# Head norms whose sums and roots stand in a 128x256 tile and are spread again by half-array products, the gating read from PSUM, and new sequences for TensorE

## The chip, the cores and the metric

The kernel runs on one core of one Trainium2 chip. The metric is the device time of one execution in microseconds (us), from the first to the last instruction and what the runtime adds around them. TensorE (PE in the profile) multiplies; PEld is its weight load, which can overlap a running product. ScalarE (ACT), VectorE (DVE) and GpSimd (POOL) work beside it, and SyncE (SP) issues the weight transfers.

## The reference

Two blocks follow each other on a sequence of 256 tokens of width 1024. The first block has two layers: a short gated convolution beside a gated DeltaNet of 8 heads (layer 0), and HGRN2 with 16 heads (layer 1). The second block has one mixer with 16 heads of width 64 (softmax attention, mLSTM, block attention) and an MLP of width 2816. All is float32. What the change touches are the norms of heads of width 128 in the first block:

```python
def rms_norm(x, g):
    xf = x.astype(jnp.float32)
    y = xf * lax.rsqrt(jnp.mean(jnp.square(xf), axis=-1, keepdims=True) + NORM_EPS)
    return (y * g.astype(jnp.float32)).astype(x.dtype)

def l2_normalize(x):
    xf = x.astype(jnp.float32)
    return (xf * lax.rsqrt(jnp.sum(jnp.square(xf), axis=-1, keepdims=True) + 1e-6)).astype(x.dtype)
...
    q, k = l2_normalize(q), l2_normalize(k)                                        # layer 0
    o = rms_norm(o, gdn_norm_g) * jax.nn.silu(z_b.reshape(bsz, s, h, GDN_HEAD_DIM)) # layer 0
    o = rms_norm(o, hgrn_norm_g) * jax.nn.silu(heads(z))                            # layer 1
```

## The kernel before

Activations lie with their features on the 128 partitions and the 256 tokens along the free dimension, so one head of width 128 is a tile of 128x256. The weights come in slabs of mostly 1 MB (`RAW`, a ring of 6). Each slab is split into a high and a low part: ScalarE copies it to `WH` (L1386, `split`), VectorE takes the difference to `WL` (L1799). TensorE then makes three products for each pair of a weight and an activation (`products`, L916 is the helper that issues every product: high by high, high by low, low by high). These are the rows with WH and WL; all other products are plain float32, and the trace shows each of those as two instructions.

The program is a list of named steps, such as `gp:0:3:1`. A step has a part on each engine that takes part in it. Each engine runs its parts in an order that is written out by hand in a table: `ORDER_T` for TensorE, `ORDER_S` for ScalarE, `ORDER_V` for VectorE. A part waits for the parts of other engines that it needs; `claim` makes TensorE wait until the last readers of a step's PSUM banks are done. A name that begins with `first:` is the first half of a step's products.

The steps that matter below:

- `norm:k:g`, `norm:q:g` (layer 0, group g of 4 heads, 4 times), `gr:g:p` (layer 0, output norm), `hr:g:p` (layer 1, 4 groups). TensorE multiplies the squares with a 128x128 tile of ones (`ONES`), which sums over the head's features and gives the sum on all 128 partitions: two float32 products of 512 columns for a group of 4 heads, ten groups in all. ScalarE takes ln, exp and a square over these 1024 columns (L1396, L1397, L1402), VectorE makes a Newton step and the product with the values (L1766 to L1768).
- `go`/`ho` make the head outputs in PSUM banks 0 and 1; `gq`/`hq` copy and square them on ScalarE (L1467, L1468); `gz`/`hz` gate them on VectorE.
- `gp`, `gu` and `gx` (layer 0): seven levels of a triangular inverse. `gp` and `gu` of levels 1 to 6 write products of 64 output columns into halves of the array (rows 128\*64), `gx` (L1079) are transposes.
- `hd`, `hm` (layer 1): products of 32 or 64 output columns, `ada`: products with `SCZ`, 32 output columns each, four of them side by side.
- `score:h`, `turn:h`, `pv:h` (second block, 16 heads of width 64): the scores take a 64-partition half of the array by the parity of h (rows 64\*128), the transposes L1307 the whole, `pv` a 64-column half (rows 128\*64).

```python
            def t_norm(step, kind, g):
                pe.wait_ge(scalar_done, scalar_at(kind, g, 1))
                for i in range(2):
                    last = mm(PS[:, step.banks[i], :], ONES[:], SQ[:, i, :])
                last.then_inc(tensor_done, 1)
```

Of the kernel before, what the change touches and what calls it, by code (L numbers as in the profile page):

```python
# [36 lines left out]
P = 128  # L37
# [78 lines left out]
def plan(stage):  # L116
# [165 lines left out]
    def gdn(g):  # L282
# [3 lines left out]
               later(step, "norm", "q", g, on="TSV", banks=(2, 3), readers="V"),  # L286
# [3 lines left out]
        for i in range(NL):  # L290
# [4 lines left out]
            for c in range(NT):  # L295
# [6 lines left out]
                later(step, "go", g, on="T", banks=(0, 1), readers="S", read_in=("gq", g, pieces(g, 2)[-1][0]))]  # L302
        out += [later(step, "gq", g, p, on="S") for p, _ in pieces(g, 2)]
        out += [later(step, "gz", g, on="V")]
        out += [later(step, "gr", g, p, on="TSV", banks=[2 + i for i in pairs], readers="V") for p, pairs in pieces(g, 2)]
        return out

    def norm_k(g):
        return later(step, "norm", "k", g, on="TSV", banks=(0, 1), readers="V")
# [180 lines left out]
gp:1:5:1 gx:1:4:1 gx:1:5:0 gp:1:6:0 gu:1:5:1 gu:1:6:0 gp:1:6:1 gx:1:5:1 gv:1:0 out:0:1:1 gs:1 gu:1:6:1 gks:1 out:0:0:2  # L490
gv:1:1 go:1 gr:1:0 gr:1:1 pl:0:0 out:0:1:2 first:out:0:0:3 first:out:0:1:3 out:0:0:3 out:0:1:3 xt:0:0:0 pl:0:1 ada:0:0
xt:0:0:1 ada:0:1 xt:0:1:0 ada:1:0 ada:1:1 adat:0 xt:0:1:1 first:gate:0:0:0 first:gate:0:0:1 gate:0:0:0 gate:0:0:1
first:gate:0:1:0 adat:1 xt:1:1 xt:1:0 first:gate:0:1:1 gate:0:1:0 gate:0:1:1 ada:2:0 ada:2:1 first:f:0:0 xt:1:3 adat:2
xt:1:2 first:f:0:1 f:0:0 f:0:1 first:q1:0:0 q1:0:0 first:q1:0:1 q1:0:1 first:i:0:0 hd:0 i:0:0 first:f:1:0 hm:0:0
first:i:0:1 hm:0:1 f:1:0 i:0:1 hm:0:2 first:f:1:1 f:1:1 hm:0:3 first:z1:0:0 z1:0:0 hm:0:4 first:z1:0:1 hm:0:5 z1:0:1
hm:0:6 first:q1:1:0 hc:0 q1:1:0 ho:0 first:q1:1:1 q1:1:1 hr:0:0 hd:1 first:i:1:0 first:f:2:0 i:1:0 first:i:1:1 hm:1:0
first:f:2:1 hm:1:1 i:1:1 f:2:0 hm:1:2 f:2:1 hm:1:3 first:z1:1:0 z1:1:0 hm:1:4 first:z1:1:1 z1:1:1 first:q1:2:0 hm:1:5
q1:2:0 hm:1:6 first:q1:2:1 hc:1 q1:2:1 ho:1 first:i:2:0 hr:1:0 hd:2 i:2:0 first:f:3:0 first:i:2:1 i:2:1 f:3:0 hm:2:0
first:f:3:1 first:z1:2:0 hm:2:1 f:3:1 hm:2:2 z1:2:0 hm:2:3 first:z1:2:1 hm:2:4 z1:2:1 hm:2:5 first:q1:3:0 hm:2:6
q1:3:0 hc:2 first:q1:3:1 ho:2 q1:3:1 hr:2:0 first:i:3:0 hd:3 i:3:0 hm:3:0 first:z1:3:0 first:i:3:1 i:3:1 hm:3:1 z1:3:0  # L500
ada:3:0 hm:3:2 first:z1:3:1 hm:3:3 z1:3:1 hm:3:4 ada:3:1 adat:3 hm:3:5 out:1:0:0 hm:3:6 out:1:1:0 hc:3 out:1:0:1 ho:3
out:1:1:1 hr:3:1 hr:3:0 out:1:0:2 pl:1:0 out:1:1:2 first:out:1:1:3 first:out:1:0:3 out:1:0:3 out:1:1:3 xt:2:0:0 pl:1:1
xt:2:0:1 ada:8:0 ada:8:1 xt:2:1:0 xt:2:1:1 ada:6:0 ada:6:1 adat:8 first:gate:1:0:0 first:gate:1:0:1 gate:1:0:0
gate:1:0:1 first:gate:1:1:0 adat:6 first:gate:1:1:1 gate:1:1:0 gate:1:1:1 ada:7:0 ada:7:1 ada:9:0 ada:9:1 ada:4:0
adat:7 xt:4:1 xt:4:0 xt:4:2 xt:4:3 adat:9 ada:4:1 first:feat:8 gates:0 feat:8 gates:1 first:feat:0 qn:1:2 gcol feat:0
first:feat:1 qn:0:0 feat:1 grow:0 first:feat:2 qn:0:1 grow:1 feat:2 first:feat:3 qn:0:2 grow:2 feat:3 first:feat:4
grow:3 first:feat:6 feat:4 first:feat:5 feat:5 grow:4 feat:6 first:feat:7 qn:1:0 feat:7 first:val:0:0 qn:1:1 score:0
val:0:0 first:val:0:1 score:1 score:2 turn:0 val:0:1 first:val:1:0 turn:1 score:3 score:4 pv:0 pv:1 turn:2 val:1:0
turn:3 score:6 score:5 first:val:1:1 turn:4 pv:2 pv:3 score:8 score:7 turn:5 val:1:1 turn:6 pv:4 pv:5 turn:7 score:9
score:10 turn:8 pv:6 pv:7 score:12 score:11 turn:9 pv:8 pv:9 turn:10 score:13 mln turn:11 ada:5:0 ada:5:1 adat:4  # L510
turn:12 pv:10 pv:11 adat:5 score:15 score:14 turn:13 pv:12 pv:13 out2:0:0 turn:14 out2:1:0 turn:15 pv:14 pv:15
first:out2:0:1 first:out2:1:1 out2:0:1 out2:1:1 ada:10:0 ada:10:1 ada:11:0 adat:10 xt:5:0 xt:5:1 xt:5:2 xt:5:3
ada:11:1 ff:0 adat:11 ff:1 ff:2 ff:3 ff:5 ff:4 ff:6 ff:8 ff:7 ff:9 ff:11 ff:10 ff:12 ff:13 ff:14 ff:15 ff:16 ff:17
ff:18 ff:19 ff:21 ff:20 down:0:0 down:0:1 down:0:2 down:0:3 down:0:4 first:down:0:5 down:1:0 down:0:5 down:1:1
down:1:2 down:1:3 down:1:4 first:down:1:5 down:1:5
# [103 lines left out]
def build(nc, wst, x_in, xt_in, pt_in, wba, wga, cst_in, msk_in, vec_in, lnrow, out):  # L619
# [11 lines left out]
    with ctx:  # L631
# [282 lines left out]
        def _(pe):  # L914
# [1527 lines left out]
```

## Time and profile before

| | before |
|---|---|
| median of 3 runs | 1049.68 us (1047.58 to 1049.87) |
| span of the profiled execution | 1048.4 us |
| PE / PEld busy | 1019.6 us (97%) / 897.6 us (86%) |
| DVE / ACT busy | 752.1 us (72%) / 530.2 us (51%) |
| PE's share of the chain that ended last | 87% |

The span of the profiled execution is 1.3 us under the median of the three runs and inside their range; the page gives no other time for it. A product in the trace is longer than the time it occupies TensorE, since the next one starts before its end: what a product occupies is the distance from its start to the start of the next.

### The profile page before, as it was taken

The page shows a single profiled execution, that of the slowest core. Times are in us where ns is not written, and L with a number is a line of the kernel's source. Part 1 is how long each engine was busy: PE and PEld are TensorE (multiplying, and loading weights), DVE is VectorE, ACT ScalarE, POOL GpSimd, SP SyncE. Part 2 cuts the span into 40 slices and gives each one's busy share as a digit, 9 for nine tenths or more (in the row PEclk, how much of TensorE's full clock was granted, in tenths as well). Part 3 has the DMA queues.
Part 4 walks back from the last instruction along what each step waited for, and adds up shares of the span by engine and source line. Part 5 has one row for each costly group of instructions (what it writes and reads, how often), then busy time and mean ns, then how long its engine had stood idle before and what let it go on. Part 6 is the DMA issues. An engine that isn't in the chain of part 4 may idle for free.

```text
span 1048.4 us, 21565 instructions
## 1 busy us (share of the span) xinstructions
PE 1019.6 (97%) x9120; PEld 897.6 (86%) x9120; DVE 752.1 (72%) x1049; ACT 530.2 (51%) x590; POOL 0.5 (0%) x7
## 2 busy tenths in 40 slices
PE   9999999999999999999999999989999999999998
PEld 7999999999866798989898787659986669999986
DVE  5999957678557668677787866867986775565553
ACT  5674544483353464435555433656687564335331
POOL 0000000000000000000000000000000000000000
PEclk8999999999999999999999999999999999999999
DMA  9454343244326664425343554876352446545441
GB/s 353 162 183 161 129 154 106 97 162 161 123 81 255 236 240 167 150 83 200 122 162 122 178 185 163 320 295 241 123 181 99 161 143 260 218 184 188 157 171 47
DMA packets 26302, 181.47 MB, mean 173 GB/s; under 512 B 3040, under 2 KB 3296, under 8 KB 4960
## 3 DMA queue, kind: packets, MB, share of 16 engines
q1 hardware_dynamic: 25056, 174.66, 45.2%
q10 hardware_dynamic: 1152, 5.45, 1.4%
q8 instruction: 73, 1.20, 0.5%
q14 instruction: 21, 0.17, 0.1%
HBM read 179.04 MB, written 1.05 MB: 172 GB/s over the span
## 4 chain that ended last, share of the span: by engine, by line
PE 87%; DVE 7%; ACT 3%; DMA 2%; issue 1%; SPq 0%; DVEq 0%; ACTq 0%
PE PS L916 84%; DVE WL L1799 2%; DMA RAW<-wst 1%; ACT WH L1386 1%; PE PS L1079 1%; DMA layer<-xt 1%; DVE X L1995 1%; DVE X L1996 1%; PE PS L1157 1%; PE PS L1307 0%; DVE STAT L1977 0%; DVE X L1976 0%; DVE layer_ln L2109 0%; DVE layer L2102 0%; ACT block L1690 0%
## 5 line engine op out<-in xcount | busy, mean ns | idle before, releaser
L916 PE MATMUL PS<-XTH,WH 128*128 128x256 f32 x1392 | 403.7, 290 | 6.2 <-issue 1.5
L916 PE MATMUL PS<-XTL,WH 128*128 128x256 f32 x1392 | 394.8, 284 | 0.0
L916 PE MATMUL PS<-XTH,WL 128*128 128x256 f32 x1392 | 394.7, 284 | 0.0
L1799 DVE TENSOR_TENSOR WL<-RAW,WH 128x2048 fp32r<-128x2048 f32 x138 | 314.2, 2277 | 99.8 <-ACT WH L1386 96.4
L1386 ACT ACTIVATE WH<-RAW 128x2048 fp32r<-128x2048 f32 x138 | 262.7, 1904 | 214.2 <-PE PS L916 208.7
L916 PEld LDWEIGHTS PS<-XTH,WH 128*128 128x128 f32 x1392 | 267.8, 192 | 12.6 <-issue 3.8
L916 PEld LDWEIGHTS PS<-XTL,WH 128*128 128x128 f32 x1392 | 268.0, 193 | 1.6 <-issue 1.4
L916 PEld LDWEIGHTS PS<-XTH,WL 128*128 128x128 f32 x1392 | 267.8, 192 | 0.0
L916 PE MATMUL PS<-WH,YH 128*128 128x512 f32 x224 | 89.6, 400 | 1.1 <-DVE YL L2274 1.1
L916 PE MATMUL PS<-WH,YL 128*128 128x512 f32 x224 | 87.4, 390 | 0.0
L916 PE MATMUL PS<-WL,YH 128*128 128x512 f32 x224 | 87.3, 390 | 0.0
L916 PE MATMUL PS<-WH,XTH 128*128 128x512 f32 x160 | 64.3, 402 | 0.9 <-ACT MROW L1569 0.8
L916 PE MATMUL PS<-WL,XTH 128*128 128x512 f32 x160 | 62.5, 390 | 0.0
L916 PE MATMUL PS<-WH,XTL 128*128 128x512 f32 x160 | 62.5, 390 | 0.0
L916 PEld LDWEIGHTS PS<-WH,YH 128*128 128x128 f32 x224 | 42.1, 188 | 10.6 <-DVE YL L2274 1.3
L916 PEld LDWEIGHTS PS<-WL,YH 128*128 128x128 f32 x224 | 42.1, 188 | 9.0 <-issue 0.7
L916 PEld LDWEIGHTS PS<-WH,YL 128*128 128x128 f32 x224 | 42.0, 188 | 8.9
L916 PEld LDWEIGHTS PS<-layer 128*32 128x32 f32 (+2 forms) x1920 | 39.5, 119 | 10.2 <-issue 4.7
L1734 ACT ACT_TABLE_LOAD x36 | 46.2, 1283 | 0.8
L916 PE MATMUL PS<-layer 128*32 128x16 f32 (+3 forms) x1920 | 44.3, 198 | 1.9 <-DVE layer L2104 1.2
L1718 ACT ACTIVATE mlp<-PS 128x256 f32<-128x256 f32 x22 | 8.4, 384 | 67.0 <-PE PS L916 55.2
L916 PEld LDWEIGHTS PS<-WH,XTH 128*128 128x128 f32 x160 | 30.1, 188 | 8.0 <-ACT MROW L1569 1.0
(293 smaller groups left out, 1112.6 us busy)
## 6 DMA issues: line engine op xcount, KB each, us to landing
RAW<-wst SPq DMA_DIRECT2D x162, 1024.0 KB, 4.9
LNW<-lnrow ACTq DMA_DIRECT2D x3, 1024.0 KB, 6.7
RAW<-wst SPq DMA_DIRECT2D x4, 512.0 KB, 5.7
layer<-xt SPq DMA_DIRECT2D x2, 512.0 KB, 5.3
XR<-x ACTq DMA_DIRECT2D x1, 1024.0 KB, 4.7
out<-X SPq DMA_DIRECT2D x4, 256.0 KB, 3.3
CST<-cst ACTq DMA_DIRECT2D x1, 640.0 KB, 8.7
PT<-pt SPq DMA_DIRECT2D x1, 512.0 KB, 5.6
```

Of the source, the lines that this page charges most:

```text
L916: return pe.matmul(o, lhsT, rhs, start=start, stop=stop)
L1079: last = pe.transpose(PS[:, 2 + c, h * P:(h + 1) * P], U[:, c * HG + h, :], ident)
L1157: last = pe.transpose(PS[:, step.banks[0], o:o + P], src[:, c, k * P:(k + 1) * P], ident)
L1386: fn(WH[:, k % SPLIT_RING, 0:n], RAW[:, i % RAW_RING, 0:n], ACT.Copy).then_inc(scalar_done, 1)
L1718: fn(SG[:, j % 2, :], PS[:, bank_of("ff", j), 0:T], ACT.Silu).then_inc(scalar_done, 1)
L1734: act.preload_act_table_set(wanted)
L1799: tt(WL[:, i % RAW_RING, 0:n], RAW[:, i % RAW_RING, 0:n], as_float(WH[:, k % SPLIT_RING, 0:n]), ALU.subtract).then_inc(vector_done, 1)
L1995: link(stt(X[:, c, s], X[:, c, s], AGG[:, c, 0:1], LNW[:, 0, s], ALU.subtract, ALU.mult))
L1996: stt(X[:, c, s], X[:, c, s], RSTD[:, c:c + 1], LNW[:, 1, s], ALU.mult, ALU.add).then_inc(vector_done, 1)
```

## The change

The sum over a head's features is now written by products with 32 columns of ones into one quarter of the output partitions for each of the 4 heads: four products of 256 columns into one 128x256 tile (`head_sums`). ScalarE and VectorE take the root there, over 256 columns and not 1024. A new TensorE step (`spread:k:g`, `spread:q:g`, `grs:g`, `hrs:g`) brings each head's root back to all 128 partitions, by four products of 256 columns whose contraction runs over 64 partitions, in turn over the lower and the upper half, the lower half's into one bank and the upper half's into another. VectorE then multiplies by the spread roots, read from PSUM. The head outputs are no longer copied by ScalarE, which only squares them (`head_squares`); VectorE gates them from PSUM (`head_outputs`). `ORDER_T` is rewritten nearly throughout, in the second block's attention too; `ORDER_S` and `ORDER_V` change where these steps stand.

```diff
+            def head_sums(bank, squares):
+                for h in range(HG):
+                    last = mm(PS[h * QUAD:(h + 1) * QUAD, bank, 0:T], ONES[:, 0:QUAD], squares(h))
+                return last
+
+            def spread(o, roots):
+                for a in range(2):
+                    for b in range(2):
+                        r, s = slice(b * HD, (b + 1) * HD), b * HD + a * QUAD
+                        pick = ident[r, s:s + 1].to_broadcast([HD, P])
+                        last = mm(o(2 * b + a), pick, roots[r, :])
+                return last
 ...
             def t_norm(step, kind, g):
                 pe.wait_ge(scalar_done, scalar_at(kind, g, 1))
-                for i in range(2):
-                    last = mm(PS[:, step.banks[i], :], ONES[:], SQ[:, i, :])
-                last.then_inc(tensor_done, 1)
+                head_sums(step.banks[0], lambda h: SQ[:, h // 2, h % 2 * T:(h % 2 + 1) * T]).then_inc(tensor_done, 1)
+
+            def t_spread(step, kind, g):
+                pe.wait_ge(cst_loaded, 16)
+                pe.wait_ge(vector_done, vector_at("norm", kind, g))
+                spread(lambda h: PS[:, step.banks[h // 2], h % 2 * T:(h % 2 + 1) * T], NR).then_inc(tensor_done, 1)
 ...
-            def t_hr(step, g, p):
-                pe.wait_ge(scalar_done, scalar_at("hq", g, p))
-                for i in dict(pieces(g, HGRN_GROUPS))[p]:
-                    last = mm(PS[:, 2 + i, :], ONES[:], tiles(HS, 2 * i, 2))
-                last.then_inc(tensor_done, 1)
+            def t_hr(step, g):
+                for c in range(NT):
+                    pe.wait_ge(scalar_done, scalar_at("hq", g, c))
+                head_sums(2, lambda h: HS[:, h, :]).then_inc(tensor_done, 1)
+
+            def t_hrs(step, g):
+                pe.wait_ge(vector_done, vector_at("hr", g))
+                spread(lambda h: PS[:, step.banks[h // 2], h % 2 * T:(h % 2 + 1) * T], HS[:, 2, :]).then_inc(tensor_done, 1)
 ...
             def s_norm(kind, g):
                 act.wait_ge(tensor_done, tensor_at("norm", kind, g))
-                b = bank_of("norm", kind, g)
-                rsqrt_and_square(flat(SQ), R2[:], PS[:, b:b + 2, :].rearrange("p b n -> p (b n)"), 1.0, 1).then_inc(scalar_done, 1)
+                rsqrt_and_square(NY, N2, PS[:, bank_of("norm", kind, g), 0:T], 1.0, 1).then_inc(scalar_done, 1)
 ...
-            def s_hq(g, p):
+            def s_hq(g, c):
                 act.wait_ge(tensor_done, tensor_at("ho", g))
                 if g:
-                    act.wait_ge(vector_done, vector_at("hr", g - 1, 0))
-                outputs(HOT, HS, dict(pieces(g, HGRN_GROUPS))[p]).then_inc(scalar_done, 1)
+                    act.wait_ge(tensor_done, tensor_at("hrs", g - 1))
+                head_squares(HS, c).then_inc(scalar_done, 1)
 ...
+            def root(x, y, r2, to, scale, eps):
+                link(stt(x, x, eps / scale, r2, ALU.add, ALU.mult))
+                return stt(to, x, -1.5, y, ALU.add, ALU.mult)
 ...
+            def v_spread(kind, g):
+                dve.wait_ge(tensor_done, tensor_at("spread", kind, g))
+                to = tiles(KT if kind == "k" else QT0, g * HG, HG)
+                stt(to, to, -1.0, banks(bank_of("spread", kind, g), 2), ALU.mult, ALU.mult).then_inc(vector_done, 1)
 ...
 ORDER_T = """
-val:0:0 first:val:0:1 score:1 score:2 turn:0 val:0:1 first:val:1:0 turn:1 score:3 score:4 pv:0 pv:1 turn:2 val:1:0
+score:3 score:4 turn:2 pv:0 score:5 pv:1 score:6 val:1:0 turn:3 pv:2 val:1:1 turn:4 score:7 pv:3 score:8 turn:5
```

The rows below are the order of TensorE's instructions in the two programs, without times; names such as `layer_83`, `layer_x` and `block_85` are the buffers in which a part of the program keeps its tiles. The first place is layer 1, the norm of the heads' second group (`hr:1`, the row with ONES) and the step `hd:2` behind it (32x32). Before:

```order
L916 MATMUL PS<-WL,XTH 128x512
L916 MATMUL PS<-WH,XTL 128x512
L916 MATMUL PS<-layer_83,ONES 128x512 x2
L916 MATMUL PS<-layer_83 32x32 x32
L916 MATMUL PS<-WH,XTH 128x512
```

The same place in the changed program, with the spread at its end:

```order
L920 MATMUL PS<-WL,XTH 128x512
L920 MATMUL PS<-WH,XTL 128x512
L920 MATMUL PS<-layer_82,ONES 32x256 x4
L920 MATMUL PS<-layer_82 32x32 x32
L920 MATMUL PS<-WH,XTH 128x512
...
L920 MATMUL PS<-WH,XTL 128x512
L920 MATMUL PS<-layer_82,CST 128x256 x4
L920 MATMUL PS<-XTH,WH 128x256
```

Two wide float32 products became four narrow ones, and behind 12 products of the next slab stand the four products that spread.

The second place is layer 0, second group, levels 2 and 3 of the inverse: 64-column rows (`64x16x4`, `64x8x8`) are `gp` and `gu`, rows with CST are the transposes `gx`. Before:

```order
L1079 MATMUL PS<-CST,layer_x 128x128 x8
L916 MATMUL PS<-layer_x,layer_77 64x8x8 x8
L916 MATMUL PS<-layer_77,layer_x 64x16x4 x8
L916 MATMUL PS<-layer_77,layer_x 64x8x8 x8
L916 MATMUL PS<-layer_x,layer_77 64x8x8 x8
L1079 MATMUL PS<-CST,layer_x 128x128 x8
```

The same place in the changed program:

```order
L1101 MATMUL PS<-CST,layer_x 128x128 x4
L920 MATMUL PS<-layer_x,layer_77 64x8x8 x8
L920 MATMUL PS<-layer_77,layer_x 64x16x4 x8
L920 MATMUL PS<-layer_77,layer_x 64x8x8 x8
L1101 MATMUL PS<-CST,layer_x 128x128 x4
L920 MATMUL PS<-layer_x,layer_77 64x8x8 x8
L1101 MATMUL PS<-CST,layer_x 128x128 x4
```

The last of the four 64-column steps now stands by itself between two transposes.

The third place is the second block's attention. A score is one row of 128 and one of 256 columns, `pv` is the row with values, L1307 (L1335 in the changed program) is `turn`. Before, at `pv:6` and `pv:7`:

```order
L1307 MATMUL PS<-CST,block_85 128x128 x3
L916 MATMUL PS<-block_85,values 64x128 x6
L916 MATMUL PS<-block_85 128x128
L916 MATMUL PS<-block_85 128x256
L916 MATMUL PS<-block_85 128x128
L916 MATMUL PS<-block_85 128x256
L1307 MATMUL PS<-CST,block_85 128x128 x3
```

In the changed program, the first scores and `pv` after the pair 3 and 4:

```order
L1335 MATMUL PS<-CST,block_84 128x128 x3
L920 MATMUL PS<-block_84,values 64x128 x3
L920 MATMUL PS<-block_84 128x128
L920 MATMUL PS<-block_84 128x256
L920 MATMUL PS<-block_84,values 64x128 x3
L920 MATMUL PS<-block_84 128x128
L920 MATMUL PS<-block_84 128x256
```

Two `pv` and two scores stood together; now they alternate.

## Rows read from the trace of the kernel before

**Rows 1.** The page: busy time of the engines, and TensorE's clock in 40 slices.

```profile
PE 1019.6 (97%) x9120; PEld 897.6 (86%) x9120; DVE 752.1 (72%) x1049; ACT 530.2 (51%) x590; POOL 0.5 (0%) x7
...
PEclk8999999999999999999999999999999999999999
```

**Rows 2.** The page, the chain that ended last, by engine.

```profile
PE 87%; DVE 7%; ACT 3%; DMA 2%; issue 1%; SPq 0%; DVEq 0%; ACTq 0%
```

**Rows 3.** Waits of PE: for whom, us in total, times, longest.

```profile
PE PS L916 <- DMA RAW<-wst: 4.1, 2, 3.0
PE PS L1157 <- DVE X L1996: 2.8, 4, 0.8
...
PE PS L916 <- DVE YL L2274: 1.1, 1, 1.1
...
PE PS L1307 <- DVE block L2257: 1.0, 1, 1.0
...
PE PS L916 <- ACT layer L1499: 0.8, 1, 0.8
```

**Rows 4.** Timeline of PE at `norm:k:0`: start, us, instruction.

```profile
32.86 1.88 PE L916 MATMUL PS<-layer,ONES 128*128 128x512 f32 x4
...
34.69 0.28 PE L916 MATMUL PS<-XTL,WH 128*128 128x256 f32 x1
34.81 0.28 PE L916 MATMUL PS<-XTH,WL 128*128 128x256 f32 x1
```

**Rows 5.** Timeline of PE at `ada:2`, 16 instructions in four column groups.

```profile
364.02 0.39 PE L916 MATMUL PS<-WL,XTH 128*128 128x512 f32 x1
364.25 0.39 PE L916 MATMUL PS<-WH,XTL 128*128 128x512 f32 x1
364.56 1.93 PE L916 MATMUL PS<-RAW,SCZ 128*32 128x512 f32 x16
366.42 0.39 PE L916 MATMUL PS<-XTH,WH 128*128 128x256 f32 x1
```

**Rows 6.** Timeline of PE: two scores and two `pv` together, each a pair.

```profile
786.16 0.93 PE L916 MATMUL PS<-block 64*128 64x128 f32 x8
787.02 1.15 PE L916 MATMUL PS<-block,values 128*64 128x128 f32 x12
788.10 0.55 PE L1307 MATMUL PS<-CST,block 128*128 128x128 f32 x3
```

**Rows 7.** Timeline of PE: `score:13` by itself.

```profile
810.81 0.92 PE L916 MATMUL PS<-block 64*128 64x128 f32 x4
811.76 1.12 PE L916 MATMUL PS<-block,CST 128*128 128x512 f32 x2
```

**Rows 8.** Timeline of PE: `gp:0:4:0` by itself, then transposes.

```profile
155.61 0.28 PE L916 MATMUL PS<-XTH,WL 128*128 128x256 f32 x1
155.82 0.69 PE L916 MATMUL PS<-layer_x,layer 128*64 128x64 f32 x16
156.44 0.87 PE L1079 MATMUL PS<-CST,layer_x 128*128 128x128 f32 x6
```

**Rows 9.** Timeline of PE: two such steps together, then transposes.

```profile
166.15 0.69 PE L916 MATMUL PS<-layer,layer_x 128*64 128x64 f32 x16
166.67 0.64 PE L916 MATMUL PS<-layer_x,layer 128*64 128x64 f32 x16
167.24 1.09 PE L1079 MATMUL PS<-CST,layer_x 128*128 128x128 f32 x8
```

**Rows 10.** Timeline of PE at `ada:4:0` and `adat:7`.

```profile
697.96 1.94 PE L916 MATMUL PS<-RAW,SCZ 128*32 128x512 f32 x8 [3.04 <-DMA RAW<-wst]
699.82 1.12 PE L1196 MATMUL PS<-CST,MROW 128*128 128x128 f32 x4
700.73 1.45 PE L1157 MATMUL PS<-CST,block 128*128 128x128 f32 x9
```

**Rows 11.** Attention, 782 to 838 us: busy us of PE, PEld, DVE, ACT, POOL.

```profile
782.00:838.00 56.00, 52.83 (x325) 38.23 (x324) 39.67 (x126) 37.58 (x89) 0.00 (x0) 1.00 0.36 132
```

**Rows 12.** Groups of ACT and DVE, splits too: busy us, mean ns.

```profile
L1799 DVE TENSOR_TENSOR WL<-RAW,WH 128x2048 fp32r<-128x2048 f32 x138 | 314.2, 2277 | 99.8 <-ACT WH L1386 96.4
L1386 ACT ACTIVATE WH<-RAW 128x2048 fp32r<-128x2048 f32 x138 | 262.7, 1904 | 214.2 <-PE PS L916 208.7
...
L1718 ACT ACTIVATE mlp<-PS 128x256 f32<-128x256 f32 x22 | 8.4, 384 | 67.0 <-PE PS L916 55.2 <-DVE YL L2299 7.8 <-DVE EL L2299 3.9
L1396 ACT ACTIVATE layer<-PS,EPS 128x1024 f32<-128x1024 f32 x7 | 7.8, 1118 | 0.1
L1767 DVE SCALAR_TENSOR_TENSOR PS<-PS,R 128x1024 f32<-128x1024 f32 x7 | 8.6, 1224 | 0.0
L2182 DVE SCALAR_TENSOR_TENSOR block<-PS,block,masks 128x256 f32<-128x256 f32 x10 | 4.8, 476 | 0.0
```

More of the change, by code:

```diff
@@ L285, in gdn @@
                later(step, "gc2", g, on="V"),
-               later(step, "norm", "q", g, on="TSV", banks=(2, 3), readers="V"),
+               later(step, "norm", "q", g, on="TSV", banks=(2,), readers="V"),
+               later(step, "spread", "q", g, on="TV", banks=(2, 3), readers="V"),
                later(step, "vtr", g, on="TV", banks=(0, 1)),
@@ L301, in gdn, with both @@
                 later(step, "gv", g, 1, on="TS", banks=(3,)),
[L302 to L306, printed above, removed]
+                later(step, "go", g, on="T", banks=(0, 1), readers="SV", read_in=("gq", g, 1)),
+                later(step, "gq", g, 0, on="SV"),
+                later(step, "gq", g, 1, on="SV"),
+                later(step, "gr", g, on="TSV", banks=(2,), readers="V"),
+                later(step, "grs", g, on="T", banks=(2, 3), readers="V", read_in=("gro", g, pieces(g, 2)[-1][0]))]
+        return out + [later(step, "gro", g, p, on="V") for p, _ in pieces(g, 2)]
     def norm_k(g):
-        return later(step, "norm", "k", g, on="TSV", banks=(0, 1), readers="V")
+        def both():
+            step("norm", "k", g, on="TSV", banks=(0,), readers="V")
+            step("spread", "k", g, on="TV", banks=(0, 1), readers="V")
+        return both
     for u in conv("k", 0) + conv("v", 0):
@@ L503 @@
[L503 to L507, printed above, removed]
@@ L513 @@
-ada:11:1 ff:0 adat:11 ff:1 ff:2 ff:3 ff:5 ff:4 ff:6 ff:8 ff:7 ff:9 ff:11 ff:10 ff:12 ff:13 ff:14 ff:15 ff:16 ff:17
-ff:18 ff:19 ff:21 ff:20 down:0:0 down:0:1 down:0:2 down:0:3 down:0:4 first:down:0:5 down:1:0 down:0:5 down:1:1
-down:1:2 down:1:3 down:1:4 first:down:1:5 down:1:5
+ba first:k:0:0 k:0:0 first:k:0:1 k:0:1 first:v:0:0 v:0:0 first:v:0:1 norm:k:0 v:0:1 first:q:0:0 spread:k:0 gcc q:0:0
+first:q:0:1 gc:0 q:0:1 first:zb:0:0 zb:0:0 first:zb:0:1 zb:0:1 first:k:1:0 k:1:0 norm:q:0 vtr:0 first:k:1:1 k:1:1
@@ new lines @@
+first:val:1:1 turn:6 score:9 pv:4 pv:5 score:10 turn:7 turn:8 ada:5:0 pv:6 pv:7 score:12 score:11 turn:9 pv:8 turn:10
+pv:9 score:13 adat:4 mln turn:11 pv:10 ada:5:1 turn:12 adat:5 pv:11 score:14 turn:13 score:15 pv:12 pv:13 out2:0:0
+turn:14 out2:1:0 turn:15 pv:14 pv:15 first:out2:0:1 first:out2:1:1 out2:0:1 out2:1:1 ada:10:0 ada:10:1 ada:11:0 adat:10
+xt:5:0 xt:5:1 xt:5:3 xt:5:2 ada:11:1 ff:0 adat:11 ff:1 ff:2 ff:3 ff:5 ff:4 ff:6 ff:8 ff:7 ff:9 ff:11 ff:10 ff:12 ff:13
+ff:14 ff:15 ff:16 ff:17 ff:18 ff:19 ff:21 ff:20 down:0:0 down:0:1 down:0:2 down:0:3 down:0:4 down:0:5 first:down:0:5
@@ L516 @@
+down:1:0 down:1:1 down:1:2 down:1:3 down:1:4 first:down:1:5 down:1:5
 """
@@ L587 @@
-split:119:145 ff:12 ff:11 ff:13 split:120:146 split:121:147 ff:14 split:122:148 split:123:149 split:124:150 ff:15
-ff:17 ff:16 split:126:152 split:125:151 ff:18 split:127:153 ff:19 split:128:154 split:129:155 split:130:156
-split:131:157 ff:20 split:132:158 ff:21 split:133:159 first:down:0:5 split:134:160 down:0:5 split:135:161
+spread:k:0 gcc v:0:1 split:6:6 q:0:0 split:7:7 q:0:1 split:8:8 gc:0 split:9:9 split:10:10 k:1:0 split:11:11 vtr:0
+norm:q:0 spread:q:0 split:12:12 k:1:1 gk:0 gc2:0 split:14:14 split:13:13 gkk:0 v:1:0 gp:0:0:0 split:15:15 gp:0:0:1
@@ L590 @@
+split:130:156 split:131:157 ff:20 split:132:158 ff:21 split:133:159 first:down:0:5 split:134:160 down:0:5 split:135:161
 split:136:162 split:137:163 split:138:164 first:down:1:5 down:1:5
@@ L1027, in t_gk @@
             def t_gk(step, g):
-                pe.wait_ge(vector_done, vector_at("norm", "k", g))
+                pe.wait_ge(vector_done, vector_at("spread", "k", g))
                 for h in range(HG):
@@ L1033, in t_gkk @@
             def t_gkk(step, g):
[L1034 removed]
+                pe.wait_ge(vector_done, vector_at("spread", "q", g))
                 for c in range(NT):
@@ L1110, in t_go, with t_gr, t_grs @@
                 last.then_inc(tensor_done, 1)
-            def t_gr(step, g, p):
-                pe.wait_ge(scalar_done, scalar_at("gq", g, p))
-                for i in dict(pieces(g, 2))[p]:
-                    last = mm(PS[:, 2 + i, :], ONES[:], tiles(SQO, 2 * i, 2))
-                last.then_inc(tensor_done, 1)
+            def t_gr(step, g):
+                for c in range(NT):
+                    pe.wait_ge(scalar_done, scalar_at("gq", g, c))
+                head_sums(2, lambda h: SQO[:, h, :]).then_inc(tensor_done, 1)
+            def t_grs(step, g):
+                pe.wait_ge(vector_done, vector_at("gr", g))
+                spread(lambda h: PS[:, step.banks[h // 2], h % 2 * T:(h % 2 + 1) * T], RO[:, 2, :]).then_inc(tensor_done, 1)
             def t_out(step, layer, n, part):
-                g, groups, name = (part, HGRN_GROUPS, "hr") if layer == 1 else (part - 2, 2, "gr")
+                g, groups, name = (part, HGRN_GROUPS, "hro") if layer == 1 else (part - 2, 2, "gro")
                 if g < 0:
```

286 lines of the change are left out of this document (140 added, 146 removed).

## The prediction

> **What bounds the kernel now.** I read the page first. TensorE is busy for 1019.6 of 1048.4 us, VectorE for 752.1 and ScalarE for 530.2, and TensorE's clock stands at 0.9 or more of full speed in all slices but the first [rows 1]. The chain that ended last runs for 87% over PE [rows 2]. Next come the waits of PE: the longest kinds are 4.1 us for weights, 2.8 us for VectorE's layer norm, then single waits of about 1 us [rows 3]. So there is no stall of tens of microseconds that narrower roots could remove. What decides is how long TensorE's own stream takes: which products, and how densely they stand. That I read from timelines of PE, by distances from start to start.
>
> **The norms' products.** Before, a group's sum is four instructions. They start at 32.86, and the second row after them starts at 34.69. One ordinary 256-column product of a weight lies between, 0.12 us as from 34.69 to 34.81; 1.83 - 0.12 = 1.71 us, so 0.428 us for each instruction of 512 float32 columns [rows 4]. Ten groups: 17.1 us.
>
> The sums of the changed kernel are four products of 32 output columns that should run side by side. `ada:2` shows that form: 16 instructions of 512 columns take from 364.56 to 366.42, 1.86 us, where 16 x 0.428 = 6.8 us would be needed one after another [rows 5]. So four column groups do run at once. With 256 columns a group's sum then takes 2 x 0.214 = 0.43 us.
>
> The spread is four products of 256 columns over half the partitions, eight instructions. The nearest rows are two scores of opposite halves, issued together: eight instructions, 2 x (2 x 128 + 2 x 256) = 1536 columns, which at 0.428 us for 512 would take 1.28 us in a row, take 786.16 to 787.02, 0.86 us [rows 6]. The halves overlap. If they do in the spread, it takes 4 x 0.214 = 0.86 us; if not, 1.71 us. I take 0.86, since its instructions alternate between halves and their results go to two banks, as those of the two scores do. Sum: (0.43 + 0.86) x 10 = 12.9 us, 4.2 us less than before.
>
> But a change between whole-array and part-array products costs time. The last product before `ada:2` starts at 364.25; a 512-column product of this kind takes 0.23 us (364.02 to 364.25), and the first narrow one starts at 364.56, 0.08 to 0.09 us late; at the end 1.86 - 4 x 0.428 = 0.15 us is over [rows 5]. Likewise 155.61 + 0.12 to 155.82 is 0.09 us [rows 8]. I take 0.10 us for each change. Twenty new part-array steps stand where ten whole-array ones stood; counted in the new sequence they add 34 changes (six are saved by neighbours that are part-array too), 3.4 us. The norms' net is -0.8 us; with changes that cost nothing it is -4.2 us, with halves that don't overlap +7.7 us.
>
> The Trainium skill ("TensorEngine Tiling (Array Packing)", Overview, Theoretical Speedup) gives up to 4 times for a dimension of 32 and up to 2 times for one of 64, and its Key Properties say that a change of tiling mode drains the engine. The table alone would make it -4.2 us; the trace has both the overlap and a fee at each change.
>
> **The rewritten order: inverse.** In layer 0 the 64-column steps stood in 20 unbroken stretches (13 and 7 for the two groups) and stand in 30 now (17 and 13). A single step occupies 155.82 to 156.44, 0.62 us and 0.09 before it [rows 8]; two together occupy 166.15 to 167.24, 1.09 and 0.09 [rows 9]. So a stretch more costs 0.71 x 2 - 1.18 = 0.24 us: +2.4 us. Below nothing it cannot be, and if these steps wait anyway it is 0. Three more `ada` stretches: +0.3 us.
>
> **The rewritten order: attention.** Before, 14 of the 16 scores stood in pairs of opposite halves. Now two pairs are left, 3 and 4, 12 and 11. A pair takes 0.86 us [rows 6], a score by itself 810.81 to 811.76, 0.95 us [rows 7]: nearly as much. Most of that is latency of four dependent loads and products, so a lone score between `pv` might take less, at least the columns' 0.64 us. I take 0.85. Before: 7 x 0.86 + 2 x 0.95 = 7.9 us. Now: 2 x 0.86 + 12 x 0.85 = 11.9 us: +4.0 (from +1.5 at 0.64 to +5.2 at 0.95). Two `pv` take 787.02 to 788.10, 1.08 us [rows 6]; alone one has six instructions of 128 columns, 6 x 0.107 = 0.64 us and about 0.1 to change: 0.74. Eight pairs were 8.6 us; four pairs and eight single ones are 10.2: +1.6.
>
> TensorE's stream: -0.8 + 2.4 + 0.3 + 4.0 + 1.6 = +7.5 us.
>
> **Waits given back.** (a) `ada:4:0` waits 3.04 us for its weights, and `adat:7` follows it for 0.9 us [rows 10]. The new order puts `adat:7` ahead, into the wait: -0.9 us. (b) In attention PE waited 1.0 us for L2257 and 1.1 us for L2274 [rows 3]; with scores and `pv` alternating, part of the 5.6 us added there falls into such waits: I take half, -1.0. (c) ScalarE and VectorE get lighter. Three passes over 1024 columns at about 1.1 us become three over 256 at about 0.4, some 2 us less for each group; on VectorE three of 1.22 become one and two of about 0.45 [rows 12]. Their work runs beside a full TensorE, so it is worth only what PE waited for them: 0.8 us for L1499, behind a norm's root [rows 3], of which I take 0.7. Sum: -2.6 us.
>
> **The new wait.** `spread` waits on VectorE's root, and everything on TensorE is queued behind it. From the sum's end to the root: 3 x 0.4 + 2 x 0.45 = 2.1 us and some semaphores. The shortest cover is in `hr:2`, one half slab of 12 products of 512 columns, 12 x 0.23 = 2.8 us. It is just enough; elsewhere 4 us or more stand between. I take 0; if a split of a slab, 1.9 us on ScalarE or 2.3 on VectorE [rows 12], got in the way at a few of the ten, it would be +5.
>
> **Sum.** 7.5 - 2.6 = +4.9 us on a span of 1048.4: 1053.3. The median of the runs is 1.3 us above that span, so in the runs' terms 1049.7 + 4.9 = 1054.6 us.
>
> **Rivals.** (1) *The added stream falls into waits.* The new order may have been laid so that what it adds stands where PE would idle. Then attention and inverse cost little: -0.8 + 2 - 2.6, about -1 to +1 us: 1049.5 us. For it: VectorE and ScalarE are busy for 40 and 38 of 56 us there and hand each head on in turns. Against: PE is idle for 56.00 - 52.83 = 3.2 us there, less than the 5.6 us added [rows 11]. (2) *Faster.* Changes cost nothing where a load can go ahead, so the norms give -4.2; breaking stretches is free; waits behind ScalarE go too, -2.6: 1043 us. Against: every row at such a change shows the 0.09 us. (3) *Much slower: halves of the spread run one after another.* The eight instructions read the same kind of broadcast column, and if the array takes them in order, each spread is 1.71 us: +8.5 us on the forecast, 1063 us. It decides as soon as the start of the second half's product is 0.2 us and not 0.01 us behind the first. Against: the scores' row. (4) *The spread's wait isn't covered*, +3 to +5 us: 1058 us; against it the covers counted above.
>
> **How the numbers follow.** Forecast and (4), slower by the stream's length: 0.62 and 0.07. (1) 0.14, (2) 0.12, (3) 0.05. What a measurement can tell from no change is 0.2%, 2.1 us. The forecast's own range is 1051 to 1059; the lower part of it and most of (1) lie within 0.2%. Slower 0.68, the same 0.19, faster 0.13. The range for 8 in 10 reaches down into (1) and up past (4): 1048.5 to 1060.
>
> **What would show it.** The row of ONES becomes 128\*32, 8 instructions for each of the ten groups, which start four at a time within 0.03 us and take 0.43 us plus a fee; the spread's 64\*128 rows start in twos. If they start one after another, (3) holds. Scores: rows of four instructions, 0.8 to 0.95 us each, and not eight in 0.93. Busy time of ACT falls by 25 us or so, of DVE by 10 to 20 us, and the end comes no earlier. PE's waits beside `spread` rows, by name of VectorE's root line, should be under 0.5 us each. The forecast is wrong if the stretch from the first score to the last `pv` is not at least 3 us longer, or if layer 0 ends earlier than before.

## The result, and the profile of the changed kernel

| | before | changed |
|---|---|---|
| median (runs) | 1048.71 us (4: 1047.58 to 1049.87) | 1063.55 us (4: 1060.35 to 1065.66) |
| ratio, 95% interval | | 1.0133 (1.0110 to 1.0157) |
| span of the profiled execution | 1048.4 us | 1063.9 us |

The changed kernel is 14.8 us slower. I had forecast +4.9 us and a range up to 1060: the direction was right, the size was three times too small. The time is the one that rival (3) gave, 1063 us, but by coincidence: its cause, halves that run one after another, is refuted below. The profiled execution of the changed kernel is the slowest of its four runs (1065.66 us), so its spans lie 15.5 us apart where the medians lie 14.8. In every run whose span is on record the time is 1.8 to 2.4 us above it, not the 1.3 that I used.

The page of the changed kernel, beside [rows 1, 2]:

```profile
PE 1034.0 (97%) x9240; PEld 906.7 (85%) x9240; DVE 737.8 (69%) x1051; ACT 504.7 (47%) x580; POOL 0.5 (0%) x7
...
PEclk8999999999999999999999989999999999999999
...
PE 86%; DVE 7%; ACT 3%; issue 2%; DMA 1%; SPq 0%; DVEq 0%; ACTq 0%
```

ScalarE and VectorE lost the 25.5 and 14.3 us they were meant to lose. TensorE, already 97% busy, gained 14.4. One digit of its clock is new: an 8 in the 24th slice, at 612 to 638 us.

The waits of TensorE (for whom, us in total, times, longest), beside [rows 3]:

```profile
PE PS L1221 <- ACT MROW L1587: 3.2, 2, 1.7
...
PE PS L920 <- DVE layer_ln L2143: 1.8, 1, 1.8
...
PE PS L920 <- DVE WL L1822: 1.7, 2, 1.5
PE PS L920 <- DVE XTL L2053: 1.6, 2, 1.2
PE PS L920 <- ACT layer L1492: 1.5, 1, 1.5
```

Some old waits went or shrank (the weights' 4.1, L2257, L1499; L1996, here L2030, from 2.8 to 1.8 us), and others of the same size came: all idle times of TensorE in the profile add up to 25.3 us, before to 23.8.

**A sum and a spread.** Timeline of PE, the sum of `norm:k:0`, beside [rows 4]:

```profile
35.57 0.28 PE L920 MATMUL PS<-XTH,WL 128*128 128x256 f32 x1
35.78 0.64 PE L920 MATMUL PS<-layer,ONES 128*32 128x256 f32 x8
36.35 0.38 PE L920 MATMUL PS<-XTH,WH 128*128 128x256 f32 x1
36.57 0.28 PE L920 MATMUL PS<-XTL,WH 128*128 128x256 f32 x1
```

and the spread `hrs:0`:

```profile
465.51 0.39 PE L920 MATMUL PS<-WH,XTL 128*128 128x512 f32 x1
465.83 1.13 PE L920 MATMUL PS<-layer,CST 64*128 64x256 f32 x8
466.89 0.39 PE L920 MATMUL PS<-XTH,WH 128*128 128x256 f32 x1
467.12 0.28 PE L920 MATMUL PS<-XTL,WH 128*128 128x256 f32 x1
```

Both kinds of overlap are there: four column groups share 0.43 us, two halves 0.86. But count what a step takes out of the stream. The product ahead of the sum is over at 35.57 + 0.12 = 35.69. The product behind it starts at 36.35, and the one after that not 0.12 but 0.22 us later; so the stream is back at 36.57 - 0.12 = 36.45. The sum occupied 0.76 us, 0.33 more than its columns. Likewise the spread: 465.74 to 467.00, 1.26 us, 0.40 more; in it the second pair of instructions also starts 0.32 us behind the first and not 0.21. The wide sum before occupied 1.71 [rows 4], and 1.81 to the start of a part-array step. So a group costs 2.02 us where it cost 1.71 to 1.81.

**Half clock.** Windows in the changed kernel around 315, 482 and 612 us (busy us of PE, PEld, DVE, ACT, POOL, then the granted clock):

```profile
308.00:315.06 7.06, 4.05 (x34) 3.23 (x33) 5.60 (x4) 3.76 (x6) 0.00 (x0) 1.00 0.27 115
315.06:318.48 3.41, 3.41 (x10) 2.64 (x9) 1.35 (x3) 0.00 (x0) 0.00 (x0) 0.50 0.00 0
...
482.32:485.73 3.41, 3.41 (x68) 3.38 (x57) 2.57 (x4) 1.60 (x2) 0.00 (x0) 0.50 0.37 149
...
612.02:618.85 6.83, 5.63 (x41) 4.71 (x42) 4.80 (x6) 0.00 (x0) 0.00 (x0) 0.50 0.74 307
```

In these three stretches TensorE was granted 1.2 and not 2.4 GHz. It was busy for 12.45 of their 13.65 us, so by these rows they cost about 6.2 us, an estimate. Before, one such stretch stands behind the first 20 us, 697.9 to 701.3, after the wait of 3.04 us [rows 10]; it falls in the middle of a slice and the page's digits hide it. What TensorE did ahead of the first one, `gr:1` and `out:0:1:2`:

```profile
309.99 0.39 PE L920 MATMUL PS<-layer 128*128 128x128 f32 x2
311.85 0.64 PE L920 MATMUL PS<-layer,ONES 128*32 128x256 f32 x8 [1.47 <-ACT layer L1492]
314.03 0.50 PE L920 MATMUL PS<-WH,YH 128*128 128x512 f32 x1 [1.55 <-DVE WL L1822]
...
315.49 0.63 PE L920 MATMUL PS<-WH,YL 128*128 128x512 f32 x1
315.91 0.63 PE L920 MATMUL PS<-WH,YH 128*128 128x512 f32 x1
```

It idled for 1.5 us twice, with 0.6 us of quarter-array work between. Behind it products of 512 columns stand 0.42 us apart, not 0.23. Before, four wide products and `pl:0:0` stood there behind one wait:

```profile
307.34 2.21 PE L916 MATMUL PS<-layer,ONES 128*128 128x512 f32 x4 [1.33 <-DVE WL L1799]
```

**Attention**, beside [rows 7] and [rows 11]:

```profile
799.76 0.92 PE L920 MATMUL PS<-block 64*128 64x128 f32 x4
800.61 0.87 PE L920 MATMUL PS<-block,values 128*64 128x128 f32 x6
801.41 0.92 PE L920 MATMUL PS<-block 64*128 64x128 f32 x4
802.26 0.50 PE L920 MATMUL PS<-WH,XTH 128*128 128x512 f32 x1
...
793.80:849.20 55.40, 53.88 (x305) 38.09 (x304) 35.88 (x124) 36.44 (x88) 0.00 (x0) 1.00 0.33 115
```

A lone score takes 0.85 us, as much as a pair did; a lone `pv` 0.80. From the end of `score:0` to the end of `turn:15` it is 65.3 us, before 59.9.

### The profile page after: what moved, and what is told of

The parts are those of the page before. It is cut to its first block, busy times and chain, and to the rows that moved or that the text cites. A ratio compares the mean times of both kernels' runs of the same rounds, so it can differ in the third digit from the quotient of the medians.

```text
span 1063.9 us, 21836 instructions
## 1 busy us (share of the span) xinstructions
PE 1034.0 (97%) x9240; PEld 906.7 (85%) x9240; DVE 737.8 (69%) x1051; ACT 504.7 (47%) x580; POOL 0.5 (0%) x7
## 4 chain that ended last, share of the span: by engine, by line
PE 86%; DVE 7%; ACT 3%; issue 2%; DMA 1%; SPq 0%; DVEq 0%; ACTq 0%
PE PS L920 83%; DVE WL L1822 2%; ACT WH L1414 1%; PE PS L1101 1%; DMA layer<-xt 1%; PE PS L1335 1%; PE PS L1182 0%; DVE block L1777 0%; PE PS L1010 0%; DVE X L2030 0%; DVE X L2029 0%; DVE X L2319 0%; DVE layer_ln L2143 0%; PE PS L1221 0%; DVE XTL L1827 0%
```

## Experiments

Ratios are to the kernel before, with 95% intervals; it was run again beside each group of experiments (medians 1049.45 to 1049.62 us). "More" and "less" are against the changed kernel's 1063.55 us.

**1. The sequence of before, with the new steps put in.** All of `ORDER_T` as before; where new steps came in (two of the places, the lines taken away are those of before):

```diff
-norm:k:0 first:v:0:1 first:q:0:0 v:0:1 gcc
+norm:k:0 first:v:0:1 first:q:0:0 v:0:1 spread:k:0 gcc
...
-gr:1:0 gr:1:1 pl:0:0 out:0:1:2 first:out:0:0:3
+gr:1 pl:0:0 out:0:1:2 grs:1 first:out:0:0:3
```

> The changed kernel with TensorE's sequence of before; only the ten sums stand where the wide sums stood, and the ten spreads are put in behind them. Theory 1 (the rewritten sequence makes the time: attention +5.1, and three stretches at half clock behind thin places in the tails of layers 0 and 1, about +6.8 less 1.7 for one that went, and waits there): within 2 us of before, 1047 to 1051. Theory 2 (the new steps themselves do it, by their changes of array form and their waits): still 1058 or more. A value between, 1051 to 1058, would share the blame.

Measured 1080.06 us, ratio 1.0304 (1.0282 to 1.0327), 16.5 above the changed kernel. By the number theory 2 holds, but neither foresaw that the old order, with the spreads put in at these places, costs more than the rewritten one, although its attention and its inverse are the cheaper ones (experiments 2 and 6): what the rewritten order gains lies elsewhere, in waits. TensorE's idle times add up to 43.0 us, against 25.3, and it ran at half clock more often (0.982 to 0.988 in the mean). Other places for the spreads were not tried. Waits of PE:

```profile
PE PS L920 <- DVE YL L1834: 5.6, 2, 3.4
PE PS L920 <- DVE layer L2124: 4.7, 1, 4.7
...
PE PS L920 <- DVE layer_x L1966: 3.5, 1, 3.5
```

**2. The attention of before.** In `ORDER_T`, all from `first:val:0:0` to `pv:15`:

```diff
-score:0 val:0:0 score:2 first:val:0:1 score:1 turn:0
+score:0 val:0:0 first:val:0:1 score:1 score:2 turn:0
```

> The changed kernel with the 63 steps of the attention in the order of before, all else as changed. Theory 1 (lone scores and pv lengthen TensorE's stream and nothing gives it back): 5.1 us less than the changed kernel's 1063.6, about 1058.4, and the time from the first score to the last pv as before. Rival (what is added falls into waits that come back without it): less than 1.5 us gained, 1062 to 1063.6.

Measured 1058.63 us, ratio 1.0090 (1.0072 to 1.0107): 4.9 less, as expected. From the end of `score:0` to the end of `turn:15` it is 60.0 us, as before. Nothing gives back what the lone scores add.

**3. `pl:0:0` moved.**

```diff
-go:1 gr:1 out:0:1:2 grs:1 pl:0:0
+go:1 gr:1 pl:0:0 out:0:1:2 grs:1
```

> The changed kernel with one step moved: pl:0:0 (8 products of 512 columns, 3.0 us) again ahead of out:0:1:2, where TensorE now idles 1.6 us for a split of VectorE. Theory 1 (the thin place makes the clock fall): the wait of 1.6 us goes and the 3.4 us at half clock behind it too, worth 1.7: 3.3 us less, about 1060.3, and no row of 0.42 us between the starts of two products of 512 columns there. Rival (only the wait counts, the clock falls for another reason): 1.6 us less, about 1062.0. If the wait only moves elsewhere: 1063.6.

Measured 1071.66 us, ratio 1.0211 (1.0193 to 1.0229): 8.1 us more, where I expected 3.3 less. Timeline of PE:

```profile
311.50 0.64 PE L920 MATMUL PS<-layer,ONES 128*32 128x256 f32 x8 [1.47 <-ACT layer L1492]
315.66 6.63 PE L920 MATMUL PS<-RAW,PT 128*128 128x512 f32 x8 [3.52 <-DVE layer_x L1966]
321.73 0.79 PE L920 MATMUL PS<-WH,YH 128*128 128x512 f32 x1
```

L1966 is `head_outputs`, the gating from PSUM. `pl:0:0` writes banks 0 and 1, which ScalarE's copy used to release before and which VectorE now holds until it has gated. The same wait of 3.5 us stands in experiment 1, which also has `pl:0:0` at this place. Then its eight products take 6.6 us where they took 3.6 before: half clock again, from 314.8 to 321.6 us. The theory of the thin place was not tested by this, since the idle time grew. So "gating from PSUM" has a price that my prediction left out: a step that filled a hole can't stand there any more.

**4. `adat:7` moved in the kernel before.**

```diff
-ada:4:0 adat:7 xt:4:1
+adat:7 ada:4:0 xt:4:1
```

> The kernel before with one step moved: adat:7 (4 products and their wait) ahead of ada:4:0, into the wait of 3.04 us for its weights. By my prediction's term (a): 0.9 us less than before, 1047.8. By the clock theory the 3.4 us at half clock behind that wait go as well, worth 1.7 us: 2.6 us less, about 1046.1.

Measured 1049.18 us (12 runs), ratio 0.9996 (0.9986 to 1.0006): nothing. Timeline of PE, beside [rows 10]:

```profile
696.71 0.63 PE L1195 MATMUL PS<-CST,MROW 128*128 128x128 f32 x4 [1.46 <-ACT MROW L1568]
698.24 1.06 PE L915 MATMUL PS<-RAW,SCZ 128*32 128x512 f32 x8 [0.90 <-DVE MODT L2043]
```

`ada:4:0` starts at 698.24, not 697.96: `adat:7` brought a wait of its own and what follows still waits, so the 0.9 us don't come. In the profiled execution no half clock follows and the span is 1.7 us shorter, but over all runs the mean granted clock is 0.995 (before 0.996), and the median is the same.

**5. Idle places filled, too much.** Products of ones ahead of five steps, and 5 more behind the sums of `gr:1`, into bank 3:

```diff
+            fill = {'gr:1': 5, 'hm:1:1': 8, 'adat:3': 7, 'out:1:0:0': 5, 'adat:7': 6}
             for step in order["T"]:
                 claim(step)
...
+                for _ in range(fill.get(":".join(map(str, step.name)), 0)):
+                    mm(PS[:, step.banks[0], 0:T], ONES[:], ONES[:].unsqueeze(1).to_broadcast([P, 2, P]))
```

> The changed kernel with products of ones (whole array, 256 columns, 0.21 us each, results never read) put into six places where TensorE idles: 5 ahead of the wait of gr:1 (1.5 us), 5 behind its sums (1.6), 8 ahead of hm:1:1 (1.8), 7 ahead of adat:3 (1.7), 5 ahead of out:1:0:0 (1.2), 6 ahead of adat:7 (1.5). They fit into the waits, so by work alone nothing changes, or it gets up to 1 us longer. Theory 1 (the idle places bring the half clock, which cost 6.8 us in the profiled execution): no stretch at half clock at 315, 482 and 612 us, and 3 to 6 us less, 1057.5 to 1060.5. Rival (the clock falls whatever stands there): 1063 to 1065.

Measured 1068.15 us, ratio 1.0185 (1.0167 to 1.0202). The clock stood at 0.996 or 0.997 in all four runs (changed kernel: 0.990 to 0.997), but each product took 0.43 us, twice what I had written, 15.4 us in all, and the eight at `hm:1:1` stood one step ahead of the wait, which stayed (1.81 us).

**6. The inverse of before, second group.** `ORDER_T` from `gkk:1` to `go:1`:

```diff
-gx:1:1:0 gp:1:2:0 out:0:0:1 gu:1:2:0 gx:1:1:1 gp:1:2:1
+gp:1:2:0 gx:1:1:0 out:0:0:1 gu:1:2:0 gp:1:2:1 gx:1:1:1
```

> The changed kernel with the steps between gkk:1 and go:1 (the inverse of the second group and what stands among it) in the order of before: 7 unbroken stretches of 64-column steps, not 13. No new step stands in this piece. By my prediction's price of 0.24 us for a stretch: the piece from gkk:1 to go:1 takes 6 x 0.24 = 1.4 us less than 64.6 us. By the two profiles (62.8 us before): 1.8 us less. Rival (those steps wait for VectorE anyway): 64 us or more.

Measured 1058.55 us, ratio 1.0101 (1.0070 to 1.0131), with runs from 1056.6 to 1064.7. The piece itself is the sharper measure: 64.59 us became 63.49. That is 1.1 us for six stretches, 0.18 each, where I had 0.24; 0.7 us above the 62.8 of before are left unexplained. The median is 5.0 less, and the piece accounts for only 1.1 of it: three of the four runs show a granted clock of 0.996 to 0.998, against 0.993 in the mean for the changed kernel.

**7. `hro` later on VectorE.**

```diff
-hd:1 hr:0 hro:0:0 split:59:66 hy:1:1
+hd:1 hr:0 split:59:66 hro:0:0 hy:1:1
```

> The changed kernel with two steps of VectorE moved: hro:0:0 behind split:59:66 and hro:1:0 behind split:67:74, since VectorE idles 2.5 us ahead of hro:0:0 for the spread and the split (2.3 us) fits in there. TensorE is unchanged. Theory 1 (VectorE's wait for the spread delays hy:1:1 and so hm:1:1, where TensorE idles 1.8 us and its clock falls): that wait falls below 0.5 us, 1.5 to 3 us less, 1060.5 to 1062. Rival (the chain of hm and hy itself is the limit): no change, 1063.6.

Measured 1060.64 us, ratio 1.0112 (1.0094 to 1.0130), 2.9 less, but not for the reason given. The wait stands as it was:

```profile
481.85 0.73 PE L920 MATMUL PS<-layer 128*32 128x16 f32 x64 [1.81 <-DVE layer_ln L2143]
```

It belongs to the chain of `hm` and `hy` in the new order. Of three half-clock stretches the profile kept one, and the mean granted clock of the runs is 0.995 against 0.993; whether the move did that or these executions were lucky is open.

**8. Each spread twice.**

```diff
-                for a in range(2):
+                for a in (0, 1, 0, 1):
                     for b in range(2):
```

> The changed kernel with each spread's eight instructions issued twice. If a spread occupies TensorE for 4 x 0.214 = 0.86 us as in my prediction and nothing covers it: 10 x 0.86 = 8.6 us more, 1072. If the halves ran one after another, 17 us more, 1080. If spreads stand in waits of TensorE for the most part: less than 5 us more, under 1068.5.

Measured 1069.74 us, ratio 1.0199 (1.0182 to 1.0217): 6.2 more, between the values expected. `hrs:0`, beside the rows at 465.83 us above:

```profile
470.03 2.00 PE L920 MATMUL PS<-layer,CST 64*128 64x256 f32 x16
471.96 0.38 PE L920 MATMUL PS<-XTH,WH 128*128 128x256 f32 x1
```

From its start to the next product it is 1.93 us and not 1.06, and so in all ten. So 0.86 us for the columns holds, and nothing covers them; that the median rose by less than 8.6 goes with less half clock in these runs (0.995 against 0.993).

**9. Filled, with the count mended.** `fill = {'gr:1': 3, 'adat:3': 3, 'adat:7': 3}` and 3 behind `gr:1`.

> As the filled kernel, with the count mended: a float32 product of 256 columns is two instructions, 0.43 us and not 0.21, so the 36 products there were 15.4 us and not 7.7, and eight of them stood where TensorE had no wait. Now 12 products, 5.1 us, all inside waits that the traces show: 3 ahead of the wait of gr:1 (1.5 us), 3 behind its sums (1.6), 3 ahead of adat:3 (1.8), 3 ahead of adat:7 (1.6). Clock theory: no half clock behind them, granted clock 0.995 to 0.997 in every run, and 1 to 3.5 us less than the changed kernel's 1063.6: 1060 to 1062.5. If filling costs as much as the clock gives: 1063 to 1065.

Measured 1060.41 us, ratio 1.0120 (1.0096 to 1.0143): 3.1 less. Timeline, then windows:

```profile
309.97 1.46 PE L920 MATMUL PS<-ONES 128*128 128x256 f32 x6
311.60 0.64 PE L920 MATMUL PS<-layer,ONES 128*32 128x256 f32 x8 [0.17 <-ACT layer L1498]
312.17 1.56 PE L920 MATMUL PS<-ONES 128*128 128x256 f32 x6
313.79 0.51 PE L920 MATMUL PS<-WH,YH 128*128 128x512 f32 x1
...
315.00:318.50 3.50, 3.50 (x18) 2.85 (x17) 1.17 (x3) 0.00 (x0) 0.00 (x0) 1.00 0.00 0
...
612.00:619.00 7.00, 7.00 (x59) 5.63 (x58) 5.81 (x8) 1.92 (x1) 0.00 (x0) 1.00 0.60 222
```

No work was taken away and some was added, and the clock stayed up in this execution. One profile proves little: that of experiment 2 has no such stretch either, without filling. The profiles of the changed kernel and its variants together say more. With the waits of 312 to 316 us open, six of eight show half clock there, filled (experiments 5, 9, 11) none of three. With the wait of `adat:3` near 610 us open, four of seven (experiment 1, with another wait there, left out), filled none of three. Behind the wait of 1.8 us near 482 us, which no filling reached, it is five of ten (experiment 1, with a longer wait, left out). The runs say the same: with filling (experiments 5, 9, 11) 12 of 16 show a mean granted clock of 0.996 or more, with the waits left open (the changed kernel, 2, 6, 7, 8, 10) 9 of 27. It is no cure: two of the six runs here took 1066.4 us at 0.993, and what held them up has no profile.

**10. The spread over the whole array.**

```diff
-                        r, s = slice(b * HD, (b + 1) * HD), b * HD + a * QUAD
-                        pick = ident[r, s:s + 1].to_broadcast([HD, P])
+                        r, s = slice(0, P), b * HD + a * QUAD
+                        pick = ident[r, s:s + 1].to_broadcast([P, P])
```

> The changed kernel with the spread over all 128 partitions: eight whole-array instructions one after another, no change of array form. Results are the same. By the traces the half-array spread occupies 1.26 us and the whole-array one would take 8 x 0.214 = 1.71: ten times 0.45 us more, 1068. If the halves bring nothing once the changes are paid, no difference: 1063.6.

Measured 1066.82 us, ratio 1.0164 (1.0151 to 1.0177): 3.3 more. `hrs:0` again:

```profile
466.63 0.39 PE L920 MATMUL PS<-WH,XTL 128*128 128x512 f32 x1
466.86 1.89 PE L920 MATMUL PS<-layer,CST 128*128 128x256 f32 x8
468.40 0.47 PE L920 MATMUL PS<-XTH,WH 128*128 128x256 f32 x1
468.70 0.28 PE L920 MATMUL PS<-XTL,WH 128*128 128x256 f32 x1
```

From 466.86 to 468.70 less one product of 0.12 it is 1.72 us: the columns and no fee. Halves are worth having, though less than their columns say: 0.46 us for each spread by the traces, of 0.86. The medians give 0.33, but these runs had less half clock than the changed kernel's (0.995 against 0.993).

**11. The changed kernel mended:** experiments 2, 6, 7 and 9 together.

> The changed kernel with all that the runs gave: the attention and the inverse of the second group in the order of before, hro:0:0 and hro:1:0 later on VectorE, the 12 filling products. Sum of the parts: 1063.6 - 5.0 - 1.1 - 3 (clock) = 1054.5, 1053 to 1056: still 4 to 7 us above before, which is what the norms' own changes of array form (+2.9) and their waits cost.

Measured 1054.10 us, ratio 1.0047 (1.0031 to 1.0063), 9.4 less. The parts add up as expected, and what is left is above before. The four medians by themselves would add up to 15.9 us: experiments 6, 7 and 9 each gained by a higher clock, and that can be had only once. In this profile two half-clock stretches of 3.4 us remain, behind the wait of `hm` (479.9 us) and behind a wait of 2.7 us for weights (712.0 us).

**12. The kernel before, filled:** `fill = {'gr:1:0': 3, 'ada:4:0': 6, 'adat:3': 2}`.

> The kernel before with 11 filling products of 0.43 us inside its waits: 3 ahead of the wait of gr:1:0 (1.4 us), 6 ahead of the weights of ada:4:0 (3.0 to 3.4), 2 ahead of adat:3 (0.9). Clock theory: half its runs show a granted clock of 0.994 to 0.995 and take 1049.5 to 1050.5, the others 0.997 and 1047 to 1048.5; filled, all show 0.997, median 1047.5 to 1048.5. Rival: no change, 1049.4.

Measured 1049.39 us (12 runs), ratio 0.9995 (0.9987 to 1.0004). Granted clocks were 0.996 or more in every run, the time did not fall: the rival was right. None of these versions beats the kernel before.

## Why the prediction failed

Two profiles are a clean pair: experiment 4 (the kernel before) and 2 (the changed one with the old attention); neither has a half-clock stretch between its first 20 us and its last 2. Their spans, 1046.7 and 1052.6, are 5.9 us apart. How much of that is waiting can't be told exactly, since a wait is counted from a modelled end: the idle times of TensorE in the two profiles, 23.0 and 25.5 us, differ by 2.4. So the first two rows below are priced by themselves, and the row of other waits is what is left of 5.9. The 15.5 us between the profiled spans divide so:

| term | predicted | measured | from |
|---|---|---|---|
| norms' products and their changes | -0.8 | +2.9 | ten groups, (0.76 + 1.26) - 1.73; at most, since three sums stand beside another part-array step |
| stretches of inverse and `ada` | +2.7 | +1.8 | ten of the inverse at 0.18, experiment 6; the three of `ada` are in the row of other waits |
| attention, waits included | +4.6 | +5.4 | 59.9 to 65.3 us; experiment 2: 4.9 |
| `adat:7` | -0.9 | 0 | experiment 4 |
| other waits of TensorE | -0.7 | +1.2 | what is left of 5.9 |
| TensorE at half clock | 0 | +4.2 | 5.9 in the changed profile (1063.9 - 1052.6 - 5.4; 6.2 by its windows) less 1.7 before |
| sum | +4.9 | +15.5 | |

- **The step that failed first** is "I take 0.10 us for each change". I read the delay of the first part-array product and stopped. At the end of a part-array step the next product starts about 0.1 us late, and its successor 0.1 us late once more. It showed before too: behind the step of [rows 5] I had found "0.15 us over" and still priced 0.10. The fee is 0.33 us for a sum and 0.40 for a spread; twenty steps cost up to 7.3 us, not 3.4, and the norms +2.9 us, not -0.8. The Trainium skill ("TensorEngine Tiling (Array Packing)", Key Properties) says that changing the tiling mode drains the engine and gives no price; these rows agree and give one.
- **The step left out** is the clock. I read the page's digits of 9 as a clock that doesn't move. Of the runs: at a mean granted clock of 0.997 the kernel before takes 1048.0 us (ten runs) and the changed one 1060.35 (one run); at 0.993, 1052.2 and 1063.5 (two and two). So at equal clock the change costs 11 to 12 us, by few runs. The rest of the 14.8 is that it runs at half clock more often: 0.993 in the mean against 0.995. Experiments 5, 9 and 11 speak for the idle places as its cause; which executions escape is open, and in the kernel before neither filling nor experiment 4 bought anything. The clock isn't all that varies either: two runs of experiment 11, both at 0.997, took 1051.88 and 1056.64 us, and that difference stays unexplained.
- **"Waits given back, -2.6"** did not come: idle times rose from 23.8 to 25.3 us. ScalarE's L1499 went (0.8 us), but `out:0:1:2` waits 1.5 us for a split that `pl:0:0` used to cover, `hm` 1.8 for VectorE, `spread:q:0` 0.4 and `hrs:1` 0.3. Rival (4), in a small form, was true. The covers I counted hold for TensorE's wait for the roots; I hadn't asked what the gating from PSUM holds (experiment 3).
- **Right**: rival (3) is false, halves and column groups overlap in all twenty steps; a lone score at 0.85 us (a lone `pv` takes 0.80, not 0.74); the attention's sum within 0.8 us; stretches of the inverse, a little dear; ScalarE's and VectorE's busy time falls and nothing of it reaches the end. Rival (1) falls with experiment 2, rival (2) with the rows of a sum and a spread.

## What to carry over

Price a change of array form by what the stream loses from the last product before it to the second one behind it, not by the first gap. When an engine is 97% busy, shorter work on the others is worth only the waits that it ends, and reading a result from PSUM with an engine that comes to it later keeps its banks from the step that would have filled the hole. Look up TensorE's granted clock by windows behind every idle place, and in every run: the page's digits hide stretches of 3.4 us, and two versions whose clocks differ can't be compared by their medians alone.

## What the runs showed of the hardware

- Eight float32 instructions of 256 columns in four column groups start within 0.02 us in fours, take 0.43 us and occupy 0.76; in two row halves they take 0.86 and occupy 1.26; over the whole array 1.72, with no fee (experiment 10).
- In the changed kernel a half-clock stretch followed two idle times of 1.5 us with 0.6 us of quarter-array work between (315 us), and one of 1.8 us (482 us); with the same idle times the profile of experiment 2 has none. A stretch lasted 3.4 or 6.8 us; experiment 3 has one of each, at 314.8 and 331.9 us.
- The same kernel, run again, can differ by 5 to 8 us, and the slower runs mostly show the lower granted clock: 1060.35 us at 0.997 and 1065.66 at 0.990 (changed kernel), 1059.38 at 0.996 and 1066.46 at 0.993 (experiment 9).
